# Backward scores kept and summed with the forward ones on GpSimd, and a mean square moved between k steps

## The reference, cut to what matters

```python
def chunked_gated_recurrence(q, k, v, log_f):
    # S_t = diag(f_t) S_{t-1} + k_t v_t^T,   o_t = S_t^T q_t
    scores = jnp.einsum('bhncd,bhnsd->bhncs', q_dec, k_intra)
    scores = jnp.where(tri_mask, scores, 0.0)
    o_intra = jnp.einsum('bhncs,bhnse->bhnce', scores, v)
    ...                                   # a scan over chunks gives o_inter

o_fwd = chunked_gated_recurrence(q, k_f, v, g_f)
o_bwd = rev(chunked_gated_recurrence(rev(q), rev(k_b), rev(v), rev(g_b)))
o = o_fwd + o_bwd
o = o * lax.rsqrt(jnp.mean(o * o, axis=-1, keepdims=True) + EPS) * hg_norm_gain
o = o * jax.nn.silu(u_g)
```

## Time and profile before

| What | us |
|---|---|
| median of 3 runs (lowest, highest) | 1643.78 (1640.47, 1647.54) |
| profiled execution, its own time | 1642.99 |
| its span, first to last instruction | 1641.4 |
| PE busy | 1534.3 (93% of the span) |
| DVE busy | 518.4 (32%) |
| ACT busy | 396.1 (24%) |
| POOL busy | 168.9 (10%) |
| mean granted clock of PE | 0.97 |

### The profile page before, as it was taken

How to read it: one execution, slowest core, us unless ns; L and a number is a source line. 1 busy time by engine, 2 the same in 40 slices (tenths; PEclk the granted TensorE clock), 3 DMA queues, 4 the chain that set the end, 5 groups by cost and what they waited for, 6 DMA issues and landing times.

```text
span 1641.4 us, 33544 instructions
## 1 busy us (share of the span) xinstructions
PE 1534.3 (93%) x14244; PEld 990.1 (60%) x14244; DVE 518.4 (32%) x1082; ACT 396.1 (24%) x578; POOL 168.9 (10%) x234
## 2 busy tenths in 40 slices
PE   8999999999989998999883999999999999999990
PEld 3444446545545554555442887777777777777860
DVE  3850044535525445434458001111111111111114
ACT  4120044455345434313440100000000000000004
POOL 2010000000000000000102011111111111111110
PEclk9999999999999999999995999999999999999995
DMA  6131132132132314434673899999999999999958
GB/s 225 39 128 65 64 135 79 64 130 84 58 118 71 123 58 162 156 138 177 229 259 128 335 315 345 355 352 355 356 357 343 373 363 364 363 367 360 383 177 319
DMA packets 76482, 364.04 MB, mean 222 GB/s; under 512 B 9816, under 2 KB 22616, under 8 KB 63216
## 3 DMA queue, kind: packets, MB, share of 16 engines
q1 hardware_dynamic: 57488, 300.90, 49.4%
q0 software_dynamic: 18336, 60.41, 12.3%
q10 hardware_dynamic: 576, 1.59, 0.3%
HBM read 299.06 MB, written 63.80 MB: 221 GB/s over the span
## 4 chain that ended last, share of the span: by engine, by line
PE 52%; DMA 3%; DVE 3%; ACT 2%; issue 1%; DVEq 0%; SPq 0%; POOLq 0%; ACTq 0%
PE bank L1801 24%; PE bank L1819 13%; PE bank L1646 7%; DMA wup<-w 2%; PE bank L1708 2%; PE bank L1791 2%; ACT junk L995 1%; PE bank L1720 1%; PE bank L1592 0%; PE bank L1726 0%; DVE wide L1275 0%; DMA x_dram<-mid,sidx 0%; PE bank L1601 0%; DMA mid<-mix_dram 0%; DMA wup<-x_dram 0%
## 5 line engine op out<-in xcount | busy, mean ns | idle before, releaser
L1801 PEld LDWEIGHTS bank<-xgT,wup 128*64 128x64 f32 (+1 forms) x7936 | 418.3, 142 | 27.9 <-issue 21.2
L1801 PE MATMUL bank<-xgT,wup 128*64 128x104 f32 (+2 forms) x7936 | 424.7, 258 | 3.8 <-issue 1.7
L1500 PE MATMUL bank<-wide,mid 128*128 128x512 f32 x960 | 423.8, 597 | 3.7 <-issue 3.7
L1500 PEld LDWEIGHTS bank<-wide,mid 128*128 128x128 f32 x960 | 180.6, 191 | 218.1 <-issue 217.2
L1819 PE MATMUL bank<-wide,hidT 128*128 128x512 f32 x544 | 239.2, 593 | 1.0 <-DVE mid L1446 1.0
L1819 PEld LDWEIGHTS bank<-wide,hidT 128*128 128x128 f32 x544 | 100.9, 191 | 115.5 <-issue 113.7
L1436 DVE TENSOR_TENSOR hidT<-sil,bank 128x512 f32<-128x512 f32 x34 | 23.4, 688 | 395.3 <-PE bank L1801 368.2
L1646 PE MATMUL bank<-early,mid 128*128 128x512 f32 x288 | 127.4, 597 | 0.0
L982 ACT ACTIVATE sil<-bank 128x512 f32<-128x512 f32 x34 | 20.3, 597 | 415.8 <-PE bank L1801 415.8
L1446 DVE TENSOR_SCALAR mid<-bank,gate_of 128x512 f32<-128x512 f32 x68 | 51.0, 751 | 205.2 <-PE bank L1819 205.1
L764 POOL DMA_INDIRECT x_dram<-mid,sidx x34 | 53.2, 1565 | 583.8 <-DVE gidx L1429 501.3
(11 more groups left out here) (225 smaller groups left out, 1254.5 us busy)
## 6 DMA issues: line engine op xcount, KB each, us to landing
wup<-w SPq DMA_DIRECT2D x68, 2048.0 KB, 17.7
wide<-w SPq DMA_DIRECT2D x34, 2048.0 KB, 10.3
u_dram<-ustage POOLq DMA_DIRECT2D x60, 256.0 KB, 2.3
rin<-u_dram SPq DMA_DIRECT2D x60, 256.0 KB, 4.3
mid<-w_in SPq DMA_DIRECT2D x23, 512.0 KB, 3.6
wide<-x_t SPq DMA_DIRECT2D x12, 512.0 KB, 11.3
mix_dram<-mixst POOLq DMA_DIRECT2D x24, 256.0 KB, 2.5
mid<-x_all SPq DMA_DIRECT2D x12, 512.0 KB, 5.4
```

The lines of the kernel that those rows point to most:

```text
L1500: last = pe.matmul(PROJ[u % 3][:, :], wsec[:, slot, k, :], nT[:, k, g * GT:(g + 1) * GT], start=(k == 0), stop=(k == KT - 1))
L1801: last = pe.matmul(bank[out_bank][c0:c0 + wide_tile, f * P:f * P + rows], weights[:, s, k, f * P + c0:f * P + c0 + wide_tile], xgT[:, k, 0 ...
```

## The change

The two buffers of masked scores (one per direction) become `scf`, one group of forward scores, and `scb`, all three groups of backward scores. In a backward step the masked scores go to `scb` and are not multiplied with the values; PE writes only state by queries to OUT. In a forward step POOL adds `scf` and the group's part of `scb` into `scsum` (which uses the storage of `wpool`, free after pooling), and PE multiplies the values with the sum. PE waits for it by a new semaphore, `scsum_ready`. POOL's addition stands first in each forward step's list, before the step's stores. The mean square of a head's last group moves from the end of the head's list to behind two k steps of the next head's first unit, of the first part (head 3) or, after head 3, behind the first half of the projection. The zeros that two early stores of ACT read are now a part of `scb`, and DVE waits for those stores (`tails_zeroed`) before it starts on the scores' bank.

```diff
-        scT = [sb(mixing, f"scT{d}", [P, BG, P]) for d in (FWD, BWD)]
+        scf = sb(mixing, "scf", [P, BG, P])
+        scb = sb(mixing, "scb", [P, NT, P])
...
-        zeros = sb(mixing, "zeros", [P, D])
+        scsum = wpool
+        zeros = scb[:, :, :].rearrange("p b c -> p (b c)")[:, 0:D]
...
-            pool.memset(zeros[:, :], 0.0)
-            for d in (FWD, BWD):
-                made(pool.memset(scT[d][:, :, :], 0.0))
+            made(pool.memset(scb[:, :, :], 0.0))
+            made(pool.memset(scf[:, :, :], 0.0))
...
+            def sum_scores(h, n):
+
+                d, g = STEPS[n]
+                if d == FWD:
+                    pool.wait_ge(st_ready, h * NS + (n + 1))
+                    pool.wait_ge(o_ready, h * NS + n)
+                    pool.tensor_tensor(scsum[:, :, :], scf[:, :, :], scb[:, g * BG:(g + 1) * BG, :],
+                                       ALU.add).then_inc(scsum_ready, 1)
...
                 for n, (d, g) in enumerate(STEPS):
+                    sum_scores(h, n)
                     if more:
...
             dve.wait_ge(consts_ready, CONSTS)
+            dve.wait_ge(tails_zeroed, 32)
...
-                dve.copy_predicated(scT[d][:, :, :], tri[d][:, :].bitcast(u32).unsqueeze(1).to_broadcast([P, BG, P]),
+                kept = scf[:, :, :] if d == FWD else scb[:, g * BG:(g + 1) * BG, :]
+                dve.copy_predicated(kept, tri[d][:, :].bitcast(u32).unsqueeze(1).to_broadcast([P, BG, P]),
...
+                if d == FWD:
+                    pe.wait_ge(scsum_ready, h * NG + (g + 1))
                 for b in range(BG):
                     cs = slice(b * P, (b + 1) * P)
-                    pe.matmul(OUT[:, cs], vtok[:, g * BG + b, :], scT[d][:, b, :], start=True, stop=False)
+                    if d == FWD:
+                        pe.matmul(OUT[:, cs], vtok[:, g * BG + b, :], scsum[:, b, :], start=True, stop=False)
                     last = pe.matmul(OUT[:, cs], state[:, b if d == FWD else b + 1, :], qint[:, cs],
-                                     start=False, stop=True)
+                                     start=(d == BWD), stop=True)
...
-                for u in range(BEFORE if more else 0):
-                    unit(h + 1, u)
-                if not more:
-                    first_part(0)
+                if more:
+                    bank_for_unit(h + 1, 0)
+                    unit_part(0, 0, 2)
+                else:
+                    bank_for_part(0)
+                    part_of_tile(0, 0, 2)
+                if not static(h, 0):
+                    mean_square(h - 1, NG - 1)
+                if more:
+                    unit_part(0, 2, KT)
+                    for u in range(1, BEFORE):
+                        unit(h + 1, u)
+                else:
+                    part_of_tile(0, 2, PK)
+                    bank_for_part(1)
+                    part_of_tile(1)
...
                     block_outputs(h, n)
-                mean_square(h, NG - 1)
...
-            for t in range(2):
-                project_half(t, t, 0)
-                project_half(t, t, 1)
+            project_half(0, 0, 0)
+            mean_square(HEADS - 1, NG - 1)
+            project_half(0, 0, 1)
+            project_half(1, 1, 0)
+            project_half(1, 1, 1)
```

More of the change, by code:

```diff
@@ L307, in trunk_program @@
         st_ready = sem("st_ready")
+        scsum_ready = sem("scsum_ready")
         o_ready = sem("o_ready")
```

## The result

The changed kernel takes 1625.81 us (median of 4 runs, 1624.98 to 1626.13) against 1645.05 us for the kernel before (4 runs, 1640.47 to 1647.54): ratio 0.9891, 95% interval 0.9879 to 0.9903. In a second comparison on another occasion it was 1627.15 against 1643.82 us, 0.990 (0.9883 to 0.9916). Faster, as forecast, but by 17 to 19 us instead of 9.4, and outside the range (1628.5 to 1641). The profiled execution took 1625.89 us, 17.1 less than the profiled one before.

What follows compares the result with a forecast made beforehand. PE's own list was taken to bound the recurrence. Terms -10.7 - 1.4 + 0.6 + 2.1 + 0 = -9.4 us took the profiled 1642.99 us to 1633.6, median forecast 1634.4, range 1628.5 to 1641.

Steps and rivals of the forecast that it cites:

- Fewer matmuls: Backward steps of the recurrence: four block-output matmuls fewer on PE, 0.89 us each in 12 steps, -10.7 us.
- The sum at no cost: Forward steps: GpSimd's sum takes 1.15 us within 8.2 us of cover before PE reads the scores, cost 0.
- Head 0 to 1: Between these heads: PE no longer idles before the moved mean square and no one is late, gain 1.4 us.
- Head 1 to 2: Loop's turn: 3.73 us idle stays, k steps run at half clock, mean square and keys come later, cost 0.6 us.
- The rival with the clock held at the turn: First rival, chance 0.20: full clock at the loop's turn, that term -2.0, total -12.0, 1631.8 us.
- Head 2 to 3: Between these heads: the mean square slips behind the load of `mixp`, keys and PE later, cost 2.1 us.
- The sign named for this, slow clock at a new place: Among the signs that would show the forecast wrong: slow clock at new places in the profile; no size given.
- Head 3 to the projection: Behind head 3: PE finishes its four halves 1.7 us sooner but then waits for the load of `mixt`, gain 0.
- The GpSimd rival: Fourth rival, chance 0.05: sum kept off operands while DVE works, late in 12 steps; slower from 9.0 us, 1656 at 10.

Runs made afterwards that it cites:

- e2: The kernel before with only the mean square moved behind two k steps, scores as before: 1639.40 us, ratio 0.9961.
- e3: The changed kernel with PE's wait for the squares put back at the end of each head's list: 1636.16 us, ratio 0.9947.
- e6: The changed kernel with the mean square behind head 3 put back ahead of the projection's first half: 1624.89 us (three runs), ratio 0.9886.
- e8: The changed kernel with each sum of scores made eight times over on GpSimd: 1668.08 us, ratio 1.0155.
- e9: The changed kernel with each sum of scores made five times over on GpSimd: 1627.69 us, ratio 0.9903.
- the parts alone: The changed kernel with the mean square put back: 1631.36 us, 0.9919; the kernel before with only the mean square moved: 1639.40 us, 0.9961.
- e4_past_branch: The kernel before with a head's last mean square made the first thing of the next head's list, behind the loop's branch: 1638.46 us, ratio 0.9962.

## Why the prediction was off, step by step

**Fewer matmuls: right.** A backward step went from 18.65 to 17.76 us and in head 3 from 25.52 to 24.63, 0.89 each as worked out. PE's chain of the changed kernel has four block outputs of a backward step (8 records) where it had eight, and then the transposes without a wait (start, length, what):

```profile
651.10 0.89 PE bank L1635 x8
651.99 0.44 PE bank L1590 x4
```

**The sum at no cost: right**, though it took longer than the 1.15 us worked out and than the 1.0 to 1.5 us named as the sign of being right: 1255 to 1612 ns, median 1568, twelve times. No run but the one with eight sums has a wait of PE for it.

**Head 0 to 1: right**, -1.6 for -1.4.

**Head 1 to 2: the step that failed.** "PE is free at 476.91, starts the product at 480.64": I took the 3.73 us of idle as the branch's own price, which would follow it wherever it stood, and the half clock with it. In fact 3.73 us is what sticks out of a branch of 4.42 us that begins only when the wait is over; begun 2.7 us before PE runs out, it took 3.71 us and left 1.29. PE started 1.29 us after it was free, at full clock, the rms came 4.2 us after that moment where I had 9.3, and the term was -5.2 instead of +0.6: 5.8 of the 7 to 10 us missed. The rival with the clock held at the turn came nearer (-2.0), but it too kept the 3.73.

**Head 2 to 3: right as a mechanism, and nearly in size.** The load was late as worked out. Four profiles with this move have the stretch at 38.8 to 39.0 us, 1.9 to 2.1 more than before, as forecast (e2, e3, e6, e8). Three have 40.1 to 40.5 (both of the changed kernel, and e9): there the clock was lower in the k steps or the mean square. I had put nothing for that. Idle time alone doesn't decide it, since PE stood 2.2 to 2.5 us ahead of the first part in most of them (1.1 in e8) with the clock up in some and down in others; what decides it isn't shown. In the changed kernel most of it came back in head 3's first step, 0.9 beyond the matmuls: the granted clock was 0.64 over 626 to 630 us and 1.00 after that, 4 us behind the first transposes, where the kernel before had 0.50 over 638 to 640 and 0.73 over 640 to 642, up to 6 us behind them. The two stretches together cost 1.4 us (64.63 to 66.08) where 2.1 less 0.9 was forecast. The sign named for this, slow clock at a new place, did show, and had little to do with the miss.

**Head 3 to the projection: open.** The times with the move undone (e6_proj_first) fit the 0, but the profiles had the stage 2.5 to 2.7 us shorter in both pairs. The 2 to 3 us that the parts alone gave beyond their stretches are open too: the start of the kernel moves by 2.4 us between profiles (228.1 to 230.5 us to the first transposes) and the stage by 2 us without a change to it, and the kernel before spreads over 8 us in its own runs. So the step that failed explains 5.8 us with its cause shown; the rest of the miss, some 2 us net by the profiles, has none.

**The range.** Its low end, 1628.5, was worked out too near: 1642.99 - 14.1 is 1628.9 already, and next to nothing was left for the runs' spread. With the turn at -5.2 instead of +0.6 the same sum gives -15.2 us and a median of 1628.6, near what was measured but still above it.

**The GpSimd rival** had the right point (about 8 us of cover) and the wrong mechanism: the sum isn't kept off for long while DVE works. With eight in a row beside a busy DVE each took 1.57 us on average (12.6 / 8), and with DVE idle 1.26.

## What to carry to other kernels

A wait as the last thing before a loop's branch costs more than itself: it keeps the engine from reaching the branch while work is still queued, so that the branch (3.3 to 5.6 us here) stands open. Look for the branch's own record, and for what the engine does while it lasts. Move the wait past the branch, even with nothing put ahead of it (e4_past_branch), and let queued work cover the branch. And before a step is moved behind other work, ask what that work waits for: behind a load, a short step on the critical chain is late with the load.

## What the runs showed of the hardware

GpSimd and VectorE got in each other's way although they touched different tiles. Groups by line of the changed kernel's `lev` product and GpSimd's sum, least, median and most ns, and then one step of its timeline:

```profile
L1162 DVE TENSOR_TENSOR lev<-keep,exk x24: 691/692/1643, 222.0 to 733.5; 128x512 f32<-128x512 f32 x24
```

```profile
L692 POOL TENSOR_TENSOR wpool<-scf,scb x12: 1255/1568/1612, 290.7 to 758.9; 128x512 f32<-128x512 f32 x12
```

```profile
310.86 0.67 DVE L1160 TENSOR_TENSOR qs<-rin,exq 128x512 f32<-128x512 f32 x1
311.05 1.61 POOL L692 TENSOR_TENSOR wpool<-scf,scb 128x512 f32<-128x512 f32 x1 [4.33 <-DVE scf L1205]
311.57 1.64 DVE L1162 TENSOR_TENSOR lev<-keep,exk 128x512 f32<-128x512 f32 x1
```

Beside an idle DVE (each head's last step) the sum took 1.26 us; here it began while DVE was in a product and took 1.61, and DVE's next product took 1.64 instead of 0.69 us and ended 0.55 us after the sum, as if it had stood until then. It is so in the first two forward steps of each head, in which DVE goes on to the next group's keys: eight of the 24 products took 1.64 us, 7.6 us more together, and DVE was busy 7 us longer in all. With five sums in a row it was busy 37 us longer (555.8 against 518.4), all of it off the path. The Trainium skill ("SBUF — State Buffer", section "SBUF: two separate sides") describes a lock on a pair of ports that these two engines share: of a VectorE instruction with two SBUF inputs and a GpSimd one, the one that starts first holds the pair for its whole instruction, and the other waits. The rows agree, in that DVE's product ended 0.55 us after the sum. They also show the pair passed on between instructions, with DVE losing more (0.95 us) than GpSimd (0.35 us) here.
